# A two-layer encoder trunk in split single precision: down projections as seven half-block products

## The reference, cut to what matters

```python
def squared_relu_mlp(h, w1, w2):          # h (512,1024), w1 (1024,4096), w2 (4096,1024)
    return jnp.square(jax.nn.relu(h @ w1)) @ w2
...
    z = jax.nn.gelu(h @ w_in); u, v = jnp.split(z, 2, axis=-1)
    v = layernorm(v, ln_g, ln_b)
    s = jnp.einsum('gpq,bnqgc->bnpgc', ws, v) + b_s.T[None, None, :, :, None]
    return (u * s) @ w_out
...
for i in range(DEPTH):
    x = x + (pool_mixer(...) if i % 2 == 0 else sgu_mixer(...))
    x = x + mem_attention(rmsnorm(x, norm_mem_g[i]), rmsnorm(mem, norm_memkv_g[i]), ...)
    x = x + squared_relu_mlp(rmsnorm(x, norm_ffn_g[i]), ffn_w1[i], ffn_w2[i])
return rmsnorm(x, final_norm_g)
```

## Time and profile before

| what | us |
|---|---|
| median of 3 runs (lowest to highest) | 1216.95 (1216.09 to 1217.52) |
| the profiled execution | 1217.14 |
| its span | 1215.3 |
| TensorE busy (share) | 1197.4 (99%) |
| VectorE busy | 661.8 (54%) |
| ScalarE busy | 398.4 (33%) |
| GpSimd busy | 177.1 (15%) |
| mean granted clock of TensorE | 0.994 |

### The profile page before, as it was taken

One profiled execution on the slowest core, in us unless ns is written; L12 is line 12 of the kernel. 1 busy time (PEld: TensorE's weight loads), 2 busy tenths in 40 slices (PEclk: granted clock), 3 DMA queues, 4 the chain that ended last, 5 costly groups with the idle time before them and its releaser, 6 DMA issues.

```text
span 1215.3 us, 14873 instructions
## 1 busy us (share of the span) xinstructions
PE 1197.4 (99%) x5538; PEld 996.5 (82%) x5538; DVE 661.8 (54%) x872; ACT 398.4 (33%) x538; POOL 177.1 (15%) x103
## 2 busy tenths in 40 slices
PE   9999999999999999999999999999999999999995
PEld 7888888888888888888888888888888888888884
DVE  7786565534534535564587565566542643534533
ACT  7655333322222212223444433343321321222210
POOL 0040053000000000160343061016000000000041
PEclk9999999999999999999999999999999999999997
DMA  9432123322222232333234422112223232232311
GB/s 372 162 117 75 35 87 121 120 89 104 97 93 98 92 104 87 104 117 126 70 105 139 156 88 100 56 39 102 92 98 104 86 104 89 101 104 86 104 36 69
DMA packets 34749, 125.34 MB, mean 103 GB/s; under 512 B 3984, under 2 KB 4112, under 8 KB 34064
## 3 DMA queue, kind: packets, MB, share of 16 engines
q1 hardware_dynamic: 33552, 121.65, 29.5%
q10 hardware_dynamic: 1152, 3.06, 0.8%
HBM read 122.59 MB, written 2.10 MB: 103 GB/s over the span
## 4 chain that ended last, share of the span: by engine, by line
PE 94%; DVE 3%; ACT 1%; POOL 0%; DMA 0%; issue 0%; DVEq 0%; ACTq 0%; POOLq 0%
PE ps L1040 29%; PE ps L1041 29%; PE ps L1042 29%; PE ps L1088 1%; PE ps L1090 1%; PE ps L1089 1%; PE ps L1229 1%; PE ps L1108 1%; DVE w_lo L669 0%; POOL sq L1029 0%; DVE out_tiles L982 0%; DMA gains<-in_gains 0%; DVE b_lo L676 0%; PE ps L1102 0%; ACT probs L559 0%
## 5 line engine op out<-in xcount | busy, mean ns | idle before, releaser
L1040 PE MATMUL ps<-a_lo,w_hi 128*128 128x512 f32 x704 | 276.4, 393 | 0.0
L441 ACT ACTIVATE w_hi<-w_raw 128x1024 fp32r<-128x1024 f32 x186 | 195.4, 1053 | 242.0 <-PE ps L1042 220.7
L1042 PE MATMUL ps<-a_hi,w_lo 128*128 128x512 f32 x704 | 274.1, 389 | 0.0
L1040 PE MATMUL ps<-b_lo,w_hi 128*128 128x512 f32 x704 | 274.0, 389 | 0.0
L1041 PE MATMUL ps<-a_hi,w_hi 128*128 128x512 f32 x704 | 274.0, 389 | 0.0
L1042 PE MATMUL ps<-b_hi,w_lo 128*128 128x512 f32 x704 | 273.9, 389 | 0.0
L1041 PE MATMUL ps<-b_hi,w_hi 128*128 128x512 f32 x704 | 273.9, 389 | 0.0
L666 DVE TENSOR_TENSOR w_lo<-w_raw,w_hi 128x1024 fp32r<-128x1024 f32 x186 | 231.6, 1247 | 21.9 <-ACT w_hi L441 21.8
L896 DVE TENSOR_TENSOR x<-ps,x 128x512 f32<-128x512 f32 x64 | 44.3, 691 | 213.5 <-PE ps L1042 195.4
L1040 PEld LDWEIGHTS ps<-a_lo,w_hi 128*128 128x128 f32 x704 | 132.2, 188 | 28.1 <-issue 1.0
L1041 PEld LDWEIGHTS ps<-a_hi,w_hi 128*128 128x128 f32 x704 | 132.2, 188 | 27.9 <-issue 1.0
(11 more groups left out here) (147 smaller groups left out, 1173.6 us busy)
## 6 DMA issues: line engine op xcount, KB each, us to landing
w_raw<-in_weights SPq DMA_DIRECT2D x218, 512.0 KB, 3.2
x<-in_x_t SPq DMA_DIRECT2D x2, 1024.0 KB, 7.8
x_tok<-in_x_rows SPq DMA_DIRECT2D x2, 1024.0 KB, 7.7
out_t<-out_tiles SPq DMA_DIRECT2D x8, 256.0 KB, 2.1
mem_raw<-in_mem_t ACTq DMA_DIRECT2D x1, 1024.0 KB, 4.8
mem_raw<-in_mem_t SPq DMA_DIRECT2D x2, 256.0 KB, 5.2
mem_raw<-in_mem_t SPq DMA_DIRECT2D x1, 512.0 KB, 6.5
ln_gain<-in_ln_g ACTq DMA_DIRECT2D x1, 512.0 KB, 3.8
```

Source lines behind the costliest of these rows:

```text
L441: act.activation(w_hi[:, slot, :], w_raw[:, slot, :], ACT.Copy, scale=row_gain(c) if b is None else 1.0).then_inc(whi_ready, 1)
L1040: pe.matmul(out_ap, s_hi, m_lo, start=start, stop=False)
L1042: return pe.matmul(out_ap, s_lo, m_hi, start=False, stop=stop)
```

## The change

Each MLP block's down part, hidden (1024) x weights (1024 x 1024), is cut in halves in tokens, hidden channels and output channels. Seven products of half blocks (256 tokens x 512 x 512) replace the eight that halves need, in a scheme that wants sums and differences of the quarters: on the activation side `n1, n2, n3, s4` beside the plain `a11, a12, a22`, on the weight side eight in-place sums of the quarters W11, W21, W12, W22 (`add_quarters`). A product is 24 matmuls, in two weight chunks of 12; the activation is stationary, the weight moves, the result is token-major and is added to a token-major accumulator `acc` (`collect`). Products P6, P7 and P4 go on accumulating in the banks of P1, P3 in those of P5. The up tiles come in the order first-half tile, second-half tile; the squared ReLU is an eviction with a maximum on VectorE and a square on ScalarE.

The raw weights get named places (`Feed`): two (R0, R1) for up chunks, eight for the quarters, which lie over the buffer b. The loops over blocks are written out. In the first MLP `acc` is turned back by 32 transposes ("xn", `turned_sums`) between the first key chunks; in the second one x is turned into `acc` by 32 transposes ("xt") behind up tiles 2 to 5. The keys of layer 1 stand directly behind the first MLP. The layer norm's gain and bias are applied behind the spatial product, with the column sums of the spatial weights ("ws_sums", one more product). The final norm works on token rows; its output is stored in four rows of 512 KB.

```diff
-PARTS = (... ("f0", 64), ("sv", 8), ("su", 8), ("k1", 8), ("v1", 8), ("so", 8), ...)
+UP, DOWN = 8, 14
+BLOCK = UP + DOWN
+PARTS = (... ("f0", BLOCK * FB), ("k1", 8), ("sv", 8), ("su", 8), ("v1", 8), ("so", 8), ...)
+PRODUCTS = ("P1", "P2", "P5", "P6", "P7", "P3", "P4")
+OPERANDS = ("n3", "a11", "a12", "a22", "n1", "n2", "s4")
+FRESH = ("P1", "P2", "P5")
+PAIR = {"P1": (0, 1), "P2": (2, 3), "P5": (4, 5), "P6": (0, 1), "P7": (0, 1), "P3": (4, 5), "P4": (0, 1)}
+SUMS = (("W11", "W12", 0), ("W11", "W12", 1), ("W12", "W22", 0), ("W12", "W22", 1),
+        ("W11", "W22", 0), ("W11", "W22", 1), ("W11", "W21", 0), ("W11", "W21", 1))
+SUM_FOR = {"P5": 0, "P7": 2, "P6": 4, "P4": 6}
...
+    def mlp(self, l):                       # class Feed: SP's loads of an MLP
+            def quarter(q, j):
+                free = ("attention", l) if b == 0 else ("wlo", base + down_chunk(b - 1, last, j) + 1)
...
+            up(0)
+            up(1)
+            for u in range(2, UP):
+                up(u)
+                quarter(*down[u - 2])
+            quarter(*down[6])
+            quarter(*down[7])
...
             def mlp(l, stat):               # ScalarE
+                hi_weights(base + AHEAD)
                 root(stat, bank(f"stat_ffn{l}"), sd, ST)
-                        hi(b_hi[:, m, :], sq[:, m % 2, :])
+                def split(b, u):
+                    first, end = (2, 7) if u % 2 else (0, 2)
+                    part = e[:, 3:8, :] if u % 2 else e[:, 0:2, :]
+                    act.wait_ge(n_ready, adds_before(l, b) + 4 * (u // 2) + (4 if u % 2 else 1))
+                    hi(h_hi[:, u // 2, first:end, :], part)
+                for b in range(FB):
+                    c = base + BLOCK * b
+                    for u in range(UP):
+                        if b or u:
+                            hi_weights(c + u + AHEAD)
+                        square(b, u)
+                        if u == UP - 1:
+                            hi_weights(c + UP + AHEAD)
+                        split(b, u)
...
             def mlp(l, stat):               # VectorE
+                def evict(b, u):
+                    dve.scalar_tensor_tensor(out=z[:, N.z[key] % 2, :], in0=bank(key), scalar=0.0, in1=rstd[:],
+                                             op0=ALU.max, op1=ALU.mult).then_inc(taken, 1)
+                def differences(b, u):
+                    dve.wait_ge(sq_ready, squares_before(l, b) + u + 1)
+                    if u % 2 == 0:
+                        dve.tensor_tensor(e[:, 0, :], e[:, 1, :], e[:, 2, :], ALU.subtract).then_inc(n_ready, 1)
+                    else:
+                        dve.scalar_tensor_tensor(out=e[:, 6, :], in0=e[:, 0, :], scalar=-1.0, in1=e[:, 4, :],
+                                                 op0=ALU.mult, op1=ALU.subtract).then_inc(n_ready, 1)
+                        dve.tensor_tensor(e[:, 5, :], e[:, 2, :], e[:, 4, :], ALU.subtract).then_inc(n_ready, 1)
+                        dve.tensor_tensor(e[:, 7, :], e[:, 3, :], e[:, 6, :], ALU.add).then_inc(n_ready, 1)
...
+                lo_weights(base + AHEAD)
                 spread(stat, f"stat_ffn{l}")
+                    for i in range(UP):
+                        if b or i:
+                            lo_weights(c + i + AHEAD)
+                        if i >= 5:
+                            add_quarters(b, i - 5)
+                        if i == 7:
+                            add_quarters(b, 3)
+                        evict(b, i)
+                        if i:
+                            split(b, i - 1)
+                        if l == 1 and b == 0 and 2 <= i < 2 + ST:
+                            turned_rows(i - 2)
+                        differences(b, i)
+                    lo_weights(d + 3)
+                    split(b, UP - 1)
+                    collect(b, "P1")
+                    lo_weights(d + 4)
+                    lo_weights(d + 5)
+                    add_quarters(b, 4)
+                    collect(b, "P2")
+                    add_quarters(b, 5)
+                    lo_weights(d + 6)
+                    lo_weights(d + 7)
+                    collect(b, "P5")
+                    lo_weights(d + 8)
+                    lo_weights(d + 9)
+                    add_quarters(b, 6)
+                    collect(b, "P6")
...
+            for half in range(2):           # VectorE, behind the first MLP
+                for m in TURNED[4 * half:4 * half + 4]:
+                    dve.tensor_tensor(x[:, m, :], bank(("xn", m)), x[:, m, :], ALU.add).then_inc(taken, 1)
+                lo_weights(C["k1"] + 4 + 2 * half)
+                for m in TURNED[4 * half:4 * half + 4]:
+                    lo_residual("xg_sgu", "mix1", m, b_lo, b_hi)
+                lo_weights(C["k1"] + 5 + 2 * half)
...
             def mlp(l, stat, norm):         # TensorE
+                def part_of(b, p, j, t):
+                    for i in (2 * j, 2 * j + 1):
+                        if p == "P1":
+                            wait_split((f"e{l}{b}", 2 * i))
+                        if p == "P2":
+                            wait_split((f"e{l}{b}", 2 * i + 1))
+                        pe.matmul(bank(key), s_hi, m_lo, start=(p in FRESH and i == 0), stop=False, skip_group_check=True)
+                        pe.matmul(bank(key), s_hi, m_hi, start=False, stop=False, skip_group_check=True)
+                        last = pe.matmul(bank(key), s_lo, m_hi, start=False, stop=(i == 3), skip_group_check=True)
+                def product(b, p):
+                    for j in range(2):
+                        pe.wait_ge(wlo_ready, base + down_chunk(b, p, j) + 1)
+                        for t in range(2):
+                            if j == 0:
+                                wait_bank((f"d{l}{b}{p}", t))
+                            last = part_of(b, p, j, t)
...
-            wait_bank("stat_final")
-            bcast(7, "stat_final", ST)
```

More of the change, by code:

```diff
@@ new lines, in _ @@
+            sp.wait_ge(psum_ready, N.ready[f"fh0{FB - 1}", UP - 1] + 1)
+            sp.dma_start(mem_raw[:], mem_t).then_inc(mem_loaded[3], 16)
+            for c in range(keys + 2, len(F.loads)):
+                load(c)
+            sp.wait_ge(psum_ready, N.ready["xt", 7] + 1)
+            sp.dma_start(final_gain[:], final_d.partition_broadcast(P)).then_inc(final_loaded, 16)
+            for t in range(ST):
+                sp.wait_ge(out_dve, t + 1)
+                if t >= 2:
+                    sp.wait_ge(out_act, t - 1)
+                sp.dma_start(out[t], acc[:, t, :]).then_inc(out_stored, 16)
@@ L606, in _ @@
[L606 to L614 removed]
+            hi_weights(C["k1"] + 3)
@@ L900, in mlp @@
[L900 to L909 removed]
+                base = C[f"f{l}"]
@@ new lines, in split, with turned_rows @@
+                def split(b, u):
+                    first, end = (2, 7) if u % 2 else (0, 2)
+                    part = e[:, 3:8, :] if u % 2 else e[:, 0:2, :]
+                    lo(N.hi[f"e{l}{b}", u], h_lo[:, u // 2, first:end, :], part, h_hi[:, u // 2, first:end, :])\
+                        .then_inc(lo_ready, 1)
+                def turned_rows(t):
+                    for h in range(2):
+                        key = ("xt", 2 * t + h)
+                        dve.wait_ge(psum_ready, N.ready[key] + 1)
+                        dve.tensor_copy(acc[:, t, h * 512:h * 512 + 512], bank(key)).then_inc(taken, 1)
@@ L987, in _, with sum_squares @@
             steps = [0]
-            def sum_squares(key, tiles=KT):
-                for m in range(tiles):
+            def sum_squares(key, order=range(KT)):
+                for i, m in enumerate(order):
                     pool.wait_ge(taken, N.bank[key, m] + 1)
@@ L1305, in mlp, with turned_rows @@
-                for m in range(8):
-                    down(m, FB - 1)
+                base = C[f"f{l}"]
+                def turned_rows(t):
+                    for h in range(2):
+                        key = ("xt", 2 * t + h)
+                        wait_bank(key)
+                        for m in range(4):
+                            last = pe.transpose(bank(key)[:, m * P:(m + 1) * P], x[:, 4 * h + m, t * P:(t + 1) * P], ident[:])
+                        last.then_inc(psum_ready, 1)
```

790 lines of the change are left out of this document (505 added, 285 removed).

## The result

The changed kernel takes **1248.4 us** (median of 4 runs, 1246.4 to 1250.5) against 1217.2 before (4 runs, 1216.1 to 1217.5): ratio 1.0259, 95% interval 1.0246 to 1.0271, slower by 31 us. The prediction was 1238, range 1198 to 1257. The profiled execution has a span of 1244.9 us, 29.6 above that of before; the sum had said 20.6.

What follows compares the result with a forecast made beforehand. TensorE was taken to bound the kernel, busy 1197.4 of 1215.3 us. The terms -43.5 + 6.7 + 0.9 + 27.0 + 21.0 + 6 - 0.5 - 7 + 10 gave +20.6 on 1217.1, about 1238 us, range 1198 to 1257.

Steps and rivals of the forecast that it cites:

- -43.5 + 6.7 + 0.9 - 7: Whole kernel: 192 fewer matmuls -43.5 us, 64 added transposes +6.7, ones-times-spatial-weights product +0.9, shorter tail -7.
- The ping-pong in an up slot: MLP up part: VectorE and ScalarE wait for each other, evictions 5.25 and 5.94 us apart, eviction 7 late by 5.77.
- The size of the waits: MLP blocks: ordinary 3.9 plus 0.6 us each, six giving +27.0; the two first blocks 10.0 and 11.0, +21.0.
- The first wait: First product of an ordinary block: TensorE waits 3.9 us for hidden part 6's low half; bounds 2.1 to 5.2.
- The clock: Behind long waits: five falls to 1.2 GHz in eight, 2.0 us each, +10 us, bounds 0 to 20.
- keys +6: Moved key chunks behind the first MLP: TensorE waits for weight splits queued behind splits of x, +6 us.
- gating -0.5: Gating loop: fourth-next value chunk waits about 1.8 us where the keys' start lost 2.3; -0.5, bounds -2 to +3.
- every split contended: Moved keys: upper case with all VectorE splits slowed beside GpSimd, waits of 11 us.
- nearer the middle: Moved keys: +6 us chosen between 1 uncontended and 11 contended, since an unscaled split stayed 1.22 us beside GpSimd.
- The loads: MLP up part: 16 half-megabyte loads on SP in 43.5 us arrive in time; cost 0.
- VectorE keeps pace: Rival in the MLPs: ordinary waits vanish, first blocks' remain at 15 us; 1189 us, chance 0.20.
- The clock falls every time: Rival: eight block waits and two at the keys lower the clock, 20 us instead of 10; 1248 us, chance 0.13.

Runs made afterwards that it cites:

- e11_last: e9 with the sixth product collected where the changed kernel does it, a weight split later than in e9; 1174.2 us, ratio to before 0.9650.
- e1_act: Changed kernel, with ScalarE making the next up weights' high part between the square and the hidden tile's high part; 1195.9 us, ratio to before 0.9828.
- e7_sums2: Changed kernel with four quarter sums moved behind the last hidden split, and P6 collected one weight split earlier; 1223.2 us, ratio to before 1.0051.
- e3_fill: Changed kernel plus 12 unused matmuls (24 in a first block) ahead of the wait for hidden part 6 in the first product; 1239.5 us.
- e10_pool1: e1_act with GpSimd's squares of the new x held until VectorE has made all its low parts; 1186.8 us.
- e6_gate: e1_act, with VectorE evicting all eight spatial tiles before making the low parts of the gated tiles; 1186.4 us, ratio to before 0.9752.
- e9: e1_act with key splits reordered, the edits of e6_gate, e4_banks and e10_pool1, and the sixth product collected a weight split earlier; 1175.7 us.
- e4_banks: Changed kernel with value chunks in the banks of the first four spatial tiles and transposed keys in those of the last four; 1243.0 us.

## Why the prediction came out as it did

The forecast (slower, through an order on VectorE and ScalarE that makes the hidden part late) was the case that came; 1238 against 1248 is 10 us too low, and errors of opposite sign stand behind it: the MLPs lost 8.5 less than forecast, the middle 17.6 more.

*What would be left without any wait.* The sum's terms without waits, -43.5 + 6.7 + 0.9 - 7, say -42.9. e11_last's span is 1172.2 against 1215.3, -43.1. Read singly: the pace is 0.227, the 64 transposes move what follows them by 6.5 us (forecast 6.7), and the tail measured 10.5 us from the last matmul's start (1234.36) to the end, against 11 forecast and 18.1 before.

*The ping-pong in an up slot.* Right. Evictions follow one another by 5.20 and 5.91 us (starts 298.72, 304.64, 309.84, 315.75), against 5.25 and 5.94. The 1280-wide split takes 1.48 on VectorE (estimate 1.49). Eviction 7 starts 5.5 us behind its slot, forecast 5.8; e1_act shows that the order is the cause, by taking it away, and e7_sums2 that the sums are the other half.

*The size of the waits.* Ordinary blocks, by e3_fill: 3.8 us each without the clock (one 5.0), forecast 4.5, so 24.1 in place of 27.0. The first wait was close (3.4 us between starts beyond the pace, forecast 3.9), the second one, at P7, is 0.25 and not 0.6. First blocks: 9.1 and 6.7, and 2.5 inside the second MLP's first up part, where TensorE waits for the banks of the turned x; 18.3 in place of 21.0. I had let the copies only delay VectorE; that TensorE waits for them earlier and so waits less at the end was missed, which is part of these 2.7 us.

*The clock.* Five falls in eight waits, as I had counted; that it was five is luck, since nothing in the rows said behind which waits the clock would stay. The price of 2.0 came from the start's 18 warm matmuls. In the timeline of before the first eight distances between their starts are 0.43 us (the very first 0.59) and the last ones 0.227, and behind a wait it is much the same: behind the wait that ends at 337.96 they start 0.43 apart from 338.55 to 340.68, and 0.23 from 341.07. So the falls stretched the matmuls by 9.3 us, near the 10 of the sum. What the sum had wrong is that it added them in full: by e3_fill's blocks they cost 7.1 net, since TensorE would have waited at P7 or for a collection for part of that time. Together the MLPs cost 24.1 + 18.3 + 7.1 = 49.5 in place of 58.

*The middle.* This step failed: "keys +6" and "gating -0.5", 5.5 in all. From the changed kernel to e11_last the middle falls from 383.6 to 358.0 us; less the 2.5 of the turned x, that is 23.1. With these, -43.1 + 49.5 + 23.1 = +29.5, and the spans differ by 29.6. (The -43.1 is e11_last's own span, so the sum tests the split between MLPs and middle and not each term.)

The keys cost 11.4 (25.2 against 13.7) and not 6. TensorE's waits there add up to 6.6 us, which looks like the forecast, but between them it ran at the lower clock, and while it is late for that reason it waits less. What counts is when the last key chunk can start: at 578.21, 8.9 us later than in e11_last, measured from the first of the 60 matmuls. Its twelve matmuls then take 5.2 us instead of 2.7 at the lower clock (0.75 in the window 570 to 590), for which the sum had no term, since its five falls were all in the MLPs. So the forecast delay of the splits was 6 where it was 8.9, near the 11 of "every split contended". I had taken "nearer the middle" because the unscaled split in the earlier trace rows had stayed at 1.22. But all eight scaled splits of x stood at their contended 1.6 us. And being unscaled hadn't protected the other: in before it starts at 537.59 and GpSimd's operation only at 537.75, while in e10_pool1 two unscaled splits of the same width that meet GpSimd take 1.97 and 1.60.

The gating cost 11.0 (27.2 against 16.2): 5.7 us of waits, and half clock from 687 to about 700 (0.52). There I had looked at the value chunks' weights and not at their banks. The value chunks accumulate in the banks of spatial tiles 4 to 7, and before it was the keys that came first, in those of tiles 0 to 3. Moving the keys away uncovered this. e6_gate gives 9.5 us back.

*The loads.* The chain has 2% of transfers, where it had 0% before, and ScalarE waits for `raw_R`, 52.8 us in all. But no wait of TensorE is put down to a transfer, and e1_act, which moves none of them by itself, brings every block to the floor: 0 holds for what they cost.

*The rivals.* "VectorE keeps pace" was refuted for this order, and became true with one line moved: its 1189 was for the waits of the first blocks kept, and e1_act, which catches up there too, has 1196 with the middle's losses. "The clock falls every time", at 1248, came out at the right total mostly by luck: the clock fell behind five of the eight block waits and not all. Its falls at the keys did come; the rest of the missing time is mainly the gating, to which no rival gave a price.

What stays open: the changed kernel's four runs spread over 4 us (1246.4 to 1250.5), those of e9 and e11 over less than 0.6. The clock's falls, which come behind some waits and not behind others of equal length, would do that; e4_banks had them behind other waits than the changed kernel. That they make the spread wasn't tested, nor what decides whether the clock falls.

## What to carry to other kernels

When two engines hand work to each other several times in a slot, add up the chain of handovers, not the busy time: here 32 us of work in 43.5 was late, and work that depends on nobody (the next weights' high part) placed where the engine would wait anyway made it punctual. When a stage is moved, look at which banks the next one falls heir to, and what empties them. And where a split can run at another time than GpSimd's work, it is about half as long (2.73 us for 6.36, 1.28 for 2.28), which in the keys' stage was worth more than the reordering (9.0 us against 3.6).

## What the runs showed of the hardware

A VectorE operation of 512 elements beside a GpSimd operation took 1.6 (scaled, with a per-partition gain) to 1.76 us (a subtraction in the gating) against 0.69 alone, and a 1024-wide scaled split 2.28 against 1.28. Additions from PSUM (`x<-ps,x`, four in 2.48 us) kept their length beside it. The Trainium skill (SBUF — State Buffer, "SBUF: two separate sides") has the rule that would have sharpened my "nearer the middle": a VectorE operation with two inputs in SBUF and a GpSimd operation that reads SBUF exclude one another for a whole instruction, whichever comes first. The trace agrees by and large: the splits, with both inputs in SBUF, stretch, and the additions with one input in PSUM don't. It also shows the order. Here in the changed kernel VectorE's split comes first and keeps its 1.28 us, and GpSimd's operation takes 2.34 where others of its kind take 1.30:

```profile
568.39 1.28 DVE L873 SCALAR_TENSOR_TENSOR w_lo<-raw_X,gains,w_hi 128x1024 fp32r<-128x1024 f32 x1 [1.88 <-ACT w_hi L602]
568.48 2.34 POOL L1352 TENSOR_TENSOR ssq<-ssq,x 128x512 f32<-128x512 f32 x1
```

The granted clock fell to its lower level, 1.2 GHz, behind three of six waits of 3.2 to 3.5 us, and behind both of 6 and 8.5; in the longest of them it was already 0.54 in the window of the wait (245 to 250) in which no matmul ran. The Trainium skill (TensorE: Matmul & The Clock Gate, "Why this matters for your kernels") says that gaps between bursts bring the lower clock back. The trace agrees in five waits and shows three, of 3.2 to 3.5 us, behind which the clock stayed. Where it fell, the matmuls behind the wait were stretched by 1.4 to 1.6 us in an ordinary block and by 2.4 to 2.5 in a first one.
